# The second layer's up product as seven half products, its convolution taps on ScalarE and its additions on VectorE

## The reference

```
u = h @ w_up                          # 256 x 1024 times 1024 x 5632
u[t] = w0*u[t-1] + w1*u[t] + w2*u[t+1] + b   # per channel, over the token axis
a, g = split(u)                       # 2816 value channels, 2816 gate channels
out = (silu(g) * a) @ w_down          # 2816 x 1024
```

## Time and profile before

| | us |
|---|---|
| median of three runs | 3447.71 (3436.28 to 3449.22) |
| profiled execution, its own time | 3443.41 |
| its span | 3441.6 |
| mean granted TensorE clock | 0.963 of full speed |
| TensorE busy | 3270.9 (95% of the span) |
| VectorE busy | 895.5 (26%) |
| ScalarE busy | 690.6 (20%) |
| GpSimd busy | 494.8 (14%) |

### The profile page before, as it was taken

The page is one execution under the profiler, slowest core; times in us unless marked ns, Lnnn a source line. Parts: engine busy times, 40 slices in busy tenths (PEclk is TensorE's granted clock), DMA queues, the critical chain, the costliest instruction groups (busy, mean ns, idle before and its releaser), DMA issues.

```text
span 3441.6 us, 81881 instructions
## 1 busy us (share of the span) xinstructions
PE 3270.9 (95%) x35194; PEld 2864.1 (83%) x35195; DVE 895.5 (26%) x1990; ACT 690.6 (20%) x1505; POOL 494.8 (14%) x441
## 2 busy tenths in 40 slices
PE   7999789999999999999999999989999999999998
PEld 5886678888887788787799887778899999988888
DVE  2324745553223321114233114131000110011001
ACT  2324132221113422212211021201111211100011
POOL 1210125555221010100057010000000000000000
PEclk9999689999899999999999999989999999999999
DMA  6546012222233244343344443238999999944477
GB/s 275 197 165 233 3 49 86 85 85 86 74 104 110 96 149 141 128 138 107 110 160 159 158 135 109 88 132 336 376 381 400 387 395 380 399 153 147 140 274 292
DMA packets 94204, 638.90 MB, mean 186 GB/s; under 512 B 10720, under 2 KB 11760, under 8 KB 36480
## 3 DMA queue, kind: packets, MB, share of 16 engines
q1 hardware_dynamic: 91472, 628.62, 49.0%
q0 software_dynamic: 2608, 8.49, 0.8%
HBM read 636.02 MB, written 1.05 MB: 185 GB/s over the span
## 4 chain that ended last, share of the span: by engine, by line
PE 88%; DMA 4%; DVE 3%; issue 2%; ACT 2%; POOL 1%; SPq 0%; ACTq 0%; DVEq 0%; POOLq 0%
PE bank L1109 18%; PE bank L663 17%; PE bank L618 12%; PE bank L781 12%; PE bank L802 5%; PE bank L634 5%; PE bank L719 3%; PE bank L1069 2%; DMA ring<-in_moe_down 2%; PE bank L566 2%; DMA ring<-in_moe_up 1%; PE bank L592 1%; PE bank L1124 1%; PE bank L838 1%; PE bank L820 1%
## 5 line engine op out<-in xcount | busy, mean ns | idle before, releaser
L781 PE MATMUL bank<-PROJ,ring 128*64 128x80 f32 (+1 forms) x7424 | 484.6, 257 | 10.8 <-DMA ring<-in_moe_down 6.6
L1109 PE MATMUL bank<-MIX,ring 128*64 128x80 f32 x12544 | 471.9, 234 | 18.3 <-issue 7.5
L781 PEld LDWEIGHTS bank<-PROJ,ring 128*64 128x64 f32 (+1 forms) x7424 | 441.7, 145 | 52.4 <-DMA ring<-in_moe_down 11.8
L1109 PEld LDWEIGHTS bank<-MIX,ring 128*64 128x64 f32 x12544 | 447.0, 137 | 44.1 <-issue 37.0
L618 PE MATMUL bank<-H,ring 128*128 128x256 f32 x1856 | 407.3, 382 | 4.3 <-ACT H L1297 4.3
L618 PEld LDWEIGHTS bank<-H,ring 128*128 128x128 f32 x1856 | 354.3, 191 | 56.8 <-issue 4.7
L1109 PE MATMUL bank<-H,ring 128*128 128x256 f32 x896 | 195.3, 381 | 0.0
L1109 PEld LDWEIGHTS bank<-H,ring 128*128 128x128 f32 x896 | 171.3, 191 | 23.9 <-issue 0.3
L663 PE MATMUL bank<-H,ring 128*64 128x128 f32 (+1 forms) x1296 | 184.8, 330 | 5.8 <-ACT H L1297 5.1
L663 PE MATMUL bank<-MIX,ring 128*64 128x128 f32 (+1 forms) x1272 | 181.1, 321 | 0.8 <-DVE MIX L1884 0.8
L802 PE MATMUL bank<-H,ring 128*128 128x256 f32 x768 | 178.1, 390 | 3.9 <-ACT PROJ L1396 3.7
(11 more groups left out here) (383 smaller groups left out, 3716.8 us busy)
## 6 DMA issues: line engine op xcount, KB each, us to landing
ring<-in_moe_up SPq DMA_DIRECT2D x224, 1024.0 KB, 7.2
ring<-in_moe_down SPq DMA_DIRECT2D x128, 896.0 KB, 6.3
ring<-in_up SPq DMA_DIRECT2D x44, 1024.0 KB, 4.8
ring<-in_mod_b SPq DMA_DIRECT2D x40, 1024.0 KB, 4.9
ring<-in_tproj SPq DMA_DIRECT2D x32, 1024.0 KB, 4.8
ring<-in_proj SPq DMA_DIRECT2D x26, 1024.0 KB, 4.8
ring<-in_gates SPq DMA_DIRECT2D x24, 1024.0 KB, 4.8
ring<-in_swup SPq DMA_DIRECT2D x22, 1024.0 KB, 4.8
```

The lines of the kernel that those rows point to most:

```text
L781: mm = pe.matmul(B[bank][lo:lo + m, 0:width], w[:, k, lo:lo + m], src(s * half + k), start=s == 0 and k == 0, stop=s == 1 and k == half - 1)
L1109: mm = pe.matmul(B[(t0 + 2 * j + t) % 4][lo:lo + m, 0:n], w[:, k, t * P + lo:t * P + lo + m], src[:, k, 0:n], start=k == 0, stop=k == KT - 1)
```

## The change

`up1` becomes a seven-product stage like `swup`, with its own division of the convolution. For each unit ScalarE makes all three taps of value and gate out of `Y`: the centre tap with its bias into `CONV`, the left and the right tap, scaled only, into the upper half of `X` (columns 256 to 511 of the tiles `4 * (j % 2)` and up, which the second layer leaves unused): six instructions of 128x256. VectorE adds the left taps of value and gate in one instruction of 128x2x255 and the right taps in another, and it, not GpSimd, multiplies value and gate. GpSimd makes the weight sums. VectorE's order in a unit is `c_sums(j)`, `add(j - 1)`, `gated(j - 2)`; ScalarE's is `head(j + 1)`, Silu of `j - 1`, `make(j)`. `make(j)` waits until `gated(j - 2)` has set `ffn_hid`. `conv_ffn` keeps serving the first layer alone.

```diff
-SEVEN = ('proj0', 'wout0', 'up0', 'down0', 'proj1', 'swup')
+SEVEN = ('proj0', 'wout0', 'up0', 'down0', 'proj1', 'up1', 'swup')
+        def taps(j, w):
+
+            return CONV[:, j % 2, :, 0:T] if w == 1 else X[:, 4 * (j % 2) + w:4 * (j % 2) + w + 2, T:TC]
+
+        def tap(j, t, w):
+
+            return taps(j, w)[:, t, :]
...
-            pairs("up1", T, ("norm6_out", 0, 1))
+            seven("up1", "norm6_out")
...
+            def conv_taps():
+
+                cw = W("conv1", 2 * FT * 4)
+
+                def head(j, it):
+                    seven_head("up1", j, it)
+
+                def make(j, it):
+                    act.wait_ge(S("ffn_hid"), it * NSLOT + (FT + j + 1))
+                    for t in range(2):
+                        src = flat(seven_parts("up1", j)[0][:, 2 * t:2 * t + 2, :])
+                        col = lambda w: cw[:, bass.ds(it * (4 * NSLOT) + 4 * (t * FT + j) + w, 1)]
+                        act.activation(tap(j, t, 1), src, ACT.Identity, bias=col(3), scale=col(1))
+                        for w in (0, 2):
+                            ins = act.activation(tap(j, t, w), src, ACT.Copy, scale=col(w))
+                    ins.then_inc(S("conv_c"), 1)
+
+                def silu(j, it):
+                    act.wait_ge(S("conv_d"), it * NSLOT + (FT + j + 1))
+                    g = tap(j, 1, 1)
+                    act.activation(g, g, ACT.Silu).then_inc(lin_free, 2)
+
+                def step_of(j, it):
+                    seven_done("up1", j, it)
+                    if j > 0:
+                        silu(j - 1, it)
+                    make(j, it)
...
+            def conv_taps():
+
+                t0 = tile_base["up1"]
+
+                def add(j, it):
+                    dve.wait_ge(S("conv_c"), it * NSLOT + (FT + j + 1))
+                    o = taps(j, 1)[:, :, 1:T]
+                    dve.tensor_tensor(o, o, taps(j, 0)[:, :, 0:T - 1], ALU.add).then_inc(S("conv_l"), 1)
+                    dve.wait_ge(S("conv_l"), it * NSLOT + (FT + j + 1))
+                    o = taps(j, 1)[:, :, 0:T - 1]
+                    dve.tensor_tensor(o, o, taps(j, 2)[:, :, 1:T], ALU.add).then_inc(S("conv_d"), 1)
+
+                def gated(j, it):
+                    dve.wait_ge(lin_free, it * (2 * NSLOT) + (t0 + 2 * j + 2 + 4))
+                    dve.tensor_tensor(PROJ[:, bass.ds(it * (NSLOT * T) + j * T, T)], tap(j, 0, 1), tap(j, 1, 1), ALU.mult)\
+                       .then_inc(S("ffn_hid"), 1)
+
+                peel = FT % NSLOT
+                for j in range(peel):
+                    c_sums("up1", j)
+                    if j > 0:
+                        add(j - 1, 0)
+                with dve.Fori(0, FT // NSLOT) as it:
+                    for j in range(peel, peel + NSLOT):
+                        c_sums("up1", j, it)
+                        add(j - 1, it)
+                        gated(j - 2, it)
+                add(FT - 1, 0)
+                gated(FT - 2, 0)
+                gated(FT - 1, 0)
...
+            x_sums("up1", "norm6_out")
+            conv_taps()
...
-            conv_ffn(1, T)
+            pool.wait_ge(unit_done, base["wout1"] + 4)
+            w_sums("up1", 0)
+            w_sums("up1", 1)
+            with pool.Fori(0, FT // NSLOT) as it:
+                for j in range(NSLOT):
+                    sums_ahead("up1", j, it)
```

More of the change, by code:

```diff
@@ L28 @@
 MOD_A = 8
-SEVEN = ('proj0', 'wout0', 'up0', 'down0', 'proj1', 'swup')
-SEVEN_UNITS = {'proj0': 11, 'wout0': 4, 'up0': 22, 'down0': 12, 'proj1': 4, 'swup': 22}
-SEVEN_WIDTH = {'proj0': 512, 'wout0': 512, 'up0': 512, 'down0': 512, 'proj1': 512, 'swup': 256}
+SEVEN = ('proj0', 'wout0', 'up0', 'down0', 'proj1', 'up1', 'swup')
+SEVEN_UNITS = {'proj0': 11, 'wout0': 4, 'up0': 22, 'down0': 12, 'proj1': 4, 'up1': 22, 'swup': 22}
+SEVEN_WIDTH = {'proj0': 512, 'wout0': 512, 'up0': 512, 'down0': 512, 'proj1': 512, 'up1': 256, 'swup': 256}
 CHUNKS = ((0, 4), (4, 4), (8, 3))
@@ L464, in seven_parts @@
                 return d.rearrange("p (i t) -> p i t", t=n), e.rearrange("p (i t) -> p i t", t=n)
-            if name in ("up0", "swup"):
+            if name in ("up0", "up1", "swup"):
                 at = 6 * T * (q % 2)
@@ L640, in wout @@
                     fm_unit(base[name] + j, tile_base[name] + 2 * j, src, width, ready=ready if j == 0 else None, half=True)
-            def pairs(name, width, ready):
-                u0, t0, peel = base[name], tile_base[name], FT % NSLOT
-                for j in range(peel):
-                    fm_unit(u0 + j, t0 + 2 * j, H, width, ready=ready if j == 0 else None)
-                with pe.Fori(0, FT // NSLOT) as it:
-                    for j in range(peel, peel + NSLOT):
-                        fm_unit(u0 + j, t0 + 2 * j, H, width, it, 2 * NSLOT)
             def seven_unit(name, j, it=0, ready=None, tight=False, between=None):
@@ L1381, in conv_ffn @@
                     pair(j, 0)
+            def conv_taps():
[21 more added lines that the diff above has]
+                peel = FT % NSLOT
+                head(0, 0)
+                for j in range(peel):
+                    head(j + 1, 0)
+                    step_of(j, 0)
+                with act.Fori(0, FT // NSLOT - 1) as it:
+                    for j in range(peel, peel + NSLOT):
+                        head(j + 1, it)
+                        step_of(j, it)
+                for j in range(FT - NSLOT, FT):
+                    if j + 1 < FT:
+                        head(j + 1, 0)
+                    step_of(j, 0)
+                silu(FT - 1, 0)
             def mod_row(n):
@@ L2286, in sums_ahead, with gated @@
                 w_sums(name, j + 2, it)
-            def conv_ffn(l, width):
-                name = f"up{l}"
-                t0 = tile_base[name]
+            def gated():
+                t0 = tile_base["up0"]
                 def pair(j, it, ahead):
-                    if ahead and name in SEVEN:
-                        sums_ahead(name, j, it)
+                    if ahead:
+                        sums_ahead("up0", j, it)
                     pool.wait_ge(lin_free, it * (2 * NSLOT) + (t0 + 2 * j + 2 + 4))
-                    pool.tensor_tensor(PROJ[:, bass.ds(it * (NSLOT * width) + j * width, width)], CONV[:, j % 2, 0, 0:width],
-                                       CONV[:, j % 2, 1, 0:width], ALU.mult).then_inc(S("ffn_hid"), 1)
+                    pool.tensor_tensor(PROJ[:, bass.ds(it * (NSLOT * TC) + j * TC, TC)], CONV[:, j % 2, 0, 0:TC],
+                                       CONV[:, j % 2, 1, 0:TC], ALU.mult).then_inc(S("ffn_hid"), 1)
                 loops = FT // NSLOT
@@ L2304, in conv_ffn @@
                     pair(j, 0, False)
-                    if l == 0:
-                        pool.wait_ge(unit_done, seven_u("up0", j) + 1)
-                        w_sums("down0", j - loops * NSLOT)
-                if l == 0:
-                    for j in range(10):
-                        sums_ahead("down0", j)
+                    pool.wait_ge(unit_done, seven_u("up0", j) + 1)
+                    w_sums("down0", j - loops * NSLOT)
+                for j in range(10):
+                    sums_ahead("down0", j)
             def window_means(l):
@@ L2349, in _ @@
                 w_sums("up0", j)
-            conv_ffn(0, TC)
+            gated()
             for j in range(2):
```

62 lines of the change are left out of this document (25 added, 37 removed).

## The result

The changed kernel takes 3457.63 us (median of 8 runs, 3454.77 to 3459.94), the kernel before 3447.79 us in runs beside it (8 runs, 3436.28 to 3450.41). The ratio is 1.0032 with a 95% interval of 1.0023 to 1.0042: 9.8 us slower by the medians, clear of no change by its interval, and within the 0.5% that the forecast set as its bound. The forecast was 3451 with a range of 3435 to 3464. The direction was right, the size was 3.7 us where 9.8 came. Of all executions in this document one, of the kernel with `gated` one place earlier, ran at a mean granted clock of 0.737 and took 4241.08 us; the ratios leave it out.

A forecast was written before the change was run, and what follows sets the result against it. The prediction took the helper ring in up1, slowed by VectorE meeting GpSimd, as the bound. Later hidden tile 1.3, low clock 2.2 and norm 0.2 sum to 3.7 us; 3447.71 + 3.7 = 3451.4 us, range 3435 to 3464.

The forecast's parts named there:

- the ring of `make`, `add` and `gated`: Between up1's units, helpers on ScalarE and VectorE take 6.95 us a round, longer than TensorE's 6.12, and set the pace.
- the second addition: In each up1 round, VectorE's second addition waits out GpSimd's next instruction: 1.67 us against 0.68 undisturbed.
- GpSimd's instruction behind it: In up1, a GpSimd weight-sum instruction behind a VectorE instruction that holds it up grows from 1.27 to 1.59 us.
- TensorE stands still: At the down product's second half sum, TensorE waits some 6 us for the last hidden tile; sign: 5 to 8.
- a low clock: Behind the down product's stall the clock is at half for a while, costing 2.2 us.
- Ahead of the stage: In the norm before up1, weight sums run beside the residual sum, mostly hidden by TensorE: 0.2 us, nothing to 1.5.
- one of its own signs of being wrong: Ahead of up1, a norm more than 1.5 us longer would show the prediction wrong.
- `gated`, 1.1 taken: In each up1 round, VectorE's product takes 1.40 us if GpSimd has an instruction left, 0.42 if not; 1.1 assumed.
- The first addition: In each up1 round, VectorE's first addition meets a GpSimd instruction somewhere in its course: 1.2 us.
- the rival in which GpSimd "blocks in full": In up1, GpSimd loses 0.47 us instead of 0.32 per meeting: round 7.25, 10.0 us slower, 3457.7; chance 12%.
- The rounds, 21 equal ones taken: In up1, 21 rounds of 6.95 us make 146 us; the last hidden tile comes 160.9 us after the start.
- The first half sum: At the down product's start, TensorE finishes its first half sum before standing still for the last hidden tile.

The follow-up runs named there:

- the new guard: Changed kernel with the down product's first tile waiting for unit 20's sums instead of its Silu (lin_free): 3459.57 us, ratio 1.0033.
- later sums: Changed kernel with GpSimd starting the weight sums of up1's units 0 and 1 only after VectorE's residual sum: 3456.27 us, ratio 1.0026.
- the last experiment: Changed kernel with weight sums of units 0 and 1 delayed and `gated` earlier: 3433.09, 3431.90 us; also with finer down-product waits: 3432.99, 3432.00 us.
- the seven products alone: Kernel before with up1 computed by seven products, the taps and GpSimd's `gated` left where they were: 3478.68 us, ratio 1.0088.

## Why the prediction was right, and where it was short

The mechanism was right step by step: the ring of `make`, `add` and `gated` sets the pace from about the ninth unit; TensorE waits for `c_sums` (L1981); the second addition takes 1.65 us (1.67 forecast); GpSimd's instruction behind it 1.60 (1.59); TensorE stands still for 5.9 us (5 to 8) and meets a low clock for 2.55 us (2.2). Its sum, 3.7 us, was short by 5 us in the profile up to the next layer's gates (8.7) and by 7.7 at the end (11.4), for these reasons:

- **Ahead of the stage, 0.2 taken, 4.0 measured.** The step that failed: that "TensorE's norm at the low clock is slower than VectorE there". It is not: a pair of VectorE instructions with a held-up addition takes 1.41 us, and TensorE's four products 1.02. It had seen that every second instruction has two SBUF inputs and then let TensorE hide the wait without setting one time against the other; its upper bound of 1.5 was too low as well, and a norm more than 1.5 us longer was one of its own signs of being wrong. Moving the sums gave 4.2 us back in the trace.
- **`gated`, 1.1 taken, 1.50 measured.** GpSimd had always an instruction left. With it, and 0.1 less at a hop, a round is 7.2 us in place of 6.95. The first addition, 1.2 taken, is 1.75 and 0.69 in turn: 1.22 in the mean, by two cases that the sum did not have. That is the number of the rival in which GpSimd "blocks in full" (7.25), whose time of 3457.7 is nearly the measured one, but not its mechanism: the two places where that rival put its loss are `gated` and the second addition, and there GpSimd's instruction grew to 1.60 from 1.27, 0.33 us, as the earlier trace rows had it. SBUF — State Buffer, "Who interferes with whom", in the Trainium skill has the two contend and the order of issue decide who blocks; the 0.47 that the prediction worked out by it is not what the rows show there. The nearest to it is the 0.43 (1.70 against 1.27) behind a first addition that had begun ahead of GpSimd's instruction. The time agreed by chance: the rest of it came mostly from the norm and the untouched work.
- **The rounds, 21 equal ones taken.** The first `make` comes at 9.9 us (9.6 forecast). The first round is 10.3 us, since `add(0)` stands behind `c_sums(1)`, which waits for the next unit's products, and a table is loaded for the Silu (1.28 us). Then come 17 of 7.23. GpSimd is two units ahead and ends at 1331.13, so the last three run at about 4.6 us undisturbed. Together 146.9 us where 146 was forecast: three errors that nearly cancel, which is luck. The last hidden tile came 161.9 us after the start (160.9 forecast).
- **The first half sum** does not run ahead of the stall, since a guard on the banks holds it until the Silu of unit 20; the new guard showed that this costs nothing here.
- **Behind the down product** 2.6 us more came in untouched work. From the first large gate products of the layer (1444.91; 1437.08 before) to `swup` the changed kernel and the one with later sums take 322 us, the kernels before, with the earlier `gated` and with the new guard 319, a step like the 3 us of the last experiment. The traces show that it is the same thing: the two that take 322 met a clock of 0.76 in the windows above, the three others 0.88. The small gates ahead took 0.9 us less than before (7.93 against 8.83), which leaves the 1.9. What decides which clock such a stretch meets stays open.

## What to carry to other kernels

When a helper chain between units is longer than it looks, write down which instruction lets the next unit's first helper go, and what stands ahead of it in its engine's list: here two exchanged calls were worth 18 us (by the traces 16.5 ahead of the down product and 2.1 in it, and some 3 more by the clock of untouched work), more than the 16.3 us that the seven products take from TensorE, with every operation unchanged. Where VectorE adds or multiplies two SBUF tiles while GpSimd works, price each such instruction, at the worst, as "to the end of GpSimd's, and 0.3 to 0.55 us more", and look for it also in the stage ahead, where the new GpSimd work begins. Whether one engine hides another is a question of two times: compare the time per tile of the engine that is said to hide with that of the one hidden.

## What the hardware showed

- A VectorE instruction with one input from a bank is not held up by GpSimd (0.41 us between two of 1.16), one with two SBUF inputs can be: 1.16 us in place of 0.41 in the norm, 1.65 or 1.75 in place of 0.69 in the additions, 1.50 in place of 0.42 in `gated`. It isn't always: an addition that began 0.14 us ahead of GpSimd's instruction kept its 0.69, and GpSimd's took 1.70 in place of 1.27; and of the taps of 128x255 beside weight sums (the seven products alone) the median is 0.48 us.
- The granted clock can fall to its lower level (1.2 GHz, 0.50) while TensorE is busy throughout, in stretches with small products in them, and for a different length in different kernels, though the products are the same: 0.76 against 0.53 in 7 us of work, and 0.76 against 0.55 in the other pair of traces. A gain of 3.4 us in one stage was taken back 650 us later in this way. The kernels differ there only in when the products arrive and in what ran before.
